# Differential attention: a unit's transposes move to right behind the next unit's scores

## The chip, the core and the metric

The kernel is one program on one core of a Trainium2 chip. The metric is the device time of one launch, in microseconds (us). The core has a matmul engine (TensorE, PE in the profile; its weight loads are listed apart as PEld), a vector engine (VectorE, DVE), an activation engine (ScalarE, ACT), GpSimd (POOL) and a queue engine (SyncE, SP). They run side by side, each works through its own instructions in order, and they wait for one another by semaphores: counters that one engine raises and another waits for.

## The reference

Two transformer blocks of two layers each run one after the other on 256 tokens of width 1024. The change lies in the second layer of the first block, in its differential attention: 8 heads, each with two sets of queries and keys of width 64 and one set of values of width 128. 256 own tokens ask, and 256 own plus 256 context tokens (512 keys) answer.

```python
def diff_attention(h_lat, h_ctx, w_qkv, lam, subln_g, w_o, lam_init, want_ctx):
    ...
    def attend(q, k, v):
        s = jnp.einsum('bqhjd,bkhjd->bhjqk', q, k).astype(jnp.float32) * scale
        p = jax.nn.softmax(s, axis=-1)
        a = p[:, :, 0] - lam_full * p[:, :, 1]
        return jnp.einsum('bhqk,bkhe->bqhe', a.astype(v.dtype), v)
```

Ahead of it come three projections (`q, k, v = jnp.split(h @ w_qkv, 3, axis=-1)`) and a rotation of queries and keys by position; behind it a norm per head and the output projection.

## The kernel before

Every large projection is done as three matmuls of split operands (`mm3`, lines 2449 to 2453: rest of the weights, rest of the activations, and the high parts of both). The weights come in chunks of 128 x 2048 through a ring of three slots. ScalarE cuts the high part out of each chunk (`split_hi`, line 787) and VectorE makes the rest (`split_lo`, line 1345).

**Tiles.** The projection of the attention is a list of tiles, `QKV`: for each of four chunks of columns two q tiles (256 tokens wide), two k tiles (512 wide) and four v tiles (256 wide), 24 matmuls each. Between them stand two "rope" tiles, one matmul with a permutation (line 2863), whose product VectorE needs to rotate q or k. From the second chunk on the order is q0, q1, k0, rope q, k1, v0, rope k, v1, v2, v3. Tile i goes into one of two banks in turn, so TensorE waits ahead of it (`o_free`) until VectorE has copied tile i - 2 out.

**Units.** The attention itself is 16 units, one per head and half of the tokens. It runs between the tiles of the next chunk. A unit u passes through:

- `scores(u)`, TensorE, line 2703: 2 matmuls of 512 columns into ps_g or ps_u (four records in the profile)
- `maximum(u)`, VectorE, line 1719, then `exp(u)`, ScalarE, line 994 (signals at_e)
- `normalise(u)`, VectorE, lines 1736 to 1743: reciprocal, factor of the second set, scaling, and the difference of both sets, which writes the probabilities (signals at_p)
- `flip(u)`, TensorE, line 2712: 4 transposes of the probabilities; waits for at_p of this unit and at_c of the unit before
- `copy(u)`, ScalarE, line 982, out of the bank (signals at_c), `values(u)`, TensorE, line 2726: 4 matmuls (eight records), and `result(u)`, VectorE, line 1748

**Order.** It is written out by hand in `diff_attention` of each engine. Behind the tiles that are no rope tiles and not q0, q1, k0, k1, v0 of the first chunk stands a slot; two slots make a unit's step. In the even slot 2u TensorE does `values(u - 2)` and `scores(u)`, VectorE copies the slot's tile and then does `normalise(u - 1)` and `maximum(u)`, ScalarE does `exp(u)`. In the odd slot 2u + 1 TensorE does `flip(u - 1)`, ScalarE `copy(u - 1)`, and VectorE copies the tile and does `result(u - 2)`. So the even slots 2 to 24 (u = 1 to 12) stand behind v3 of the first chunk; then behind q1, k1, v1 and v3 in turn; the last, slot 24, behind v1 of the last chunk. The odd slots 3 to 25 stand behind q0, k0, v0 and v2. In slot 25 TensorE also does `scores(13)`; slot 26 has an order of its own (`values(11)`, `flip(12)`, `scores(14)`), and the rest follows behind the last tile.

VectorE's order in a step, with q0 to v3 in the place of the tile that it copies, is for example: copy k1, `normalise(2)`, `maximum(3)`; copy v0, `result(1)`, `split_lo`, the rotation of k (lines 1757 to 1759); copy v1, `normalise(3)`, `maximum(4)`; copy v2, `result(2)`; copy v3, and so on.

Of the kernel before, what the change touches and what calls it, by code (L numbers as in the profile page):

```python
# [199 lines left out]
def freed(tiles):  # L200

    return BANKS + tiles
# [73 lines left out]
def build(nc, W, ADA, AW, CB, XT, MEMT, VEC, CST, PM, BT, REL, LAM, W0B, LORA, GUP, OUT, stop=None):  # L276
# [13 lines left out]
    with ExitStack() as ctx:  # L290
# [319 lines left out]
        def qkv_slot(i):  # L610

            kind, c, j = QKV[i]
            if (kind, j) not in QKV_SLOT:
                return None
            s = QKV_SLOT[kind, j]
            return 8 * c + s if s < 3 else 8 * (c - 1) + s if c else None

        def qkv_last(i):

            return i + 1 == len(QKV) or QKV[i + 1][0] in "qkv" and QKV[i][0][-1:] != QKV[i + 1][0] and (QKV[i][0], QKV[i + 1][0]) not in (("rope q", "k"), ("rope k", "v"))  # L620
# [1815 lines left out]
        def _(pe):  # L2436
# [4 lines left out]
            def chunk(n, i=None, per=SLOTS):  # L2441

                pe.wait_ge(w_lo, n + 1 if i is None else i * per + (n + 1))
                return n % SLOTS

            def weights(s, cols_):
                return (whi[:, s, :].rearrange("p (k n) -> p k n", n=cols_), wlo[:, s, :].rearrange("p (k n) -> p k n", n=cols_))
# [7 lines left out]
            def keep_clock(n, bank):  # L2455

                for _ in range(n):
                    mm(bank, ones, cst[:, 0:bank.shape[-1]], start=True, stop=True)
# [233 lines left out]
            def attention(a):  # L2692
                U = ATT[a]

                def scores(u):
                    g, unit = AT0[a] + u, U[u]
                    if g >= 2:
                        pe.wait_ge(at_e, g - 1)
                    if g >= AT0[1] + 3 and is_mem(g):
                        pe.wait_ge(at_y, g - 2)  # L2700
                    bank = att_scores(g)
                    for (rows, b, c), q, k in unit["scores"]:
                        ins = mm(bank[rows, b, c], q, k, start=True, stop=True)  # L2703
                    ins.then_inc(at_s, 1)

                def flip(u):
                    g, unit = AT0[a] + u, U[u]
                    pe.wait_ge(at_p, g + 1)
                    if g:
                        pe.wait_ge(at_c, g)  # L2710
                    for b in range(unit["nb"]):
                        ins = nc.tensor.transpose(att_flip(g, b), probs[g % 2][:, b * 128:(b + 1) * 128], ident)  # L2712
                    ins.then_inc(at_t, 1)

                def values(u):
                    g, unit = AT0[a] + u, U[u]
                    pe.wait_ge(at_c, g + 1)
                    if g < DIFF_UNITS:
                        pe.wait_ge(o_free, freed(QKV_T0 + QKV_V[u // 4] + 1))
                    if g >= 2:  # L2720
                        pe.wait_ge(at_y, g - (g >= DIFF_UNITS))
                    elif g:
                        pe.wait_ge(at_y, g)
                    nb = unit["nb"]
                    for b in range(nb):
                        ins = mm(att_out(g)[unit["rows"]], unit["v"][b], probs_t[a][g % 2][:, b, :], start=b == 0, stop=b == nb - 1)  # L2726
                    ins.then_inc(at_o, 1)

                return scores, flip, values
# [109 lines left out]
            def diff_first():  # L2839

                n = FIRST["qkv", 0]
                ready = split_input(NTOK)
                w = [weights(chunk(n + b), 256) for b in range(2)]
                for i in range(4):
                    pe.wait_ge(o_free, QKV_T0 + i + 1)
                for part, half in enumerate(HALVES):
                    for k in range(KT):
                        ready(k + KT * part)
                        for i in range(2 * part, 4) if part else range(4):
                            b, c = i // 2, slice(i % 2 * 128, i % 2 * 128 + 128)  # L2850
                            ins = mm3(qkv_bank(i)[:, half], (w[b][0][:, k, c], w[b][1][:, k, c]), (hh[:, k, half], hl[:, k, half]), k == 0, k == KT - 1)
                            if k == KT - 1 and part == b:
                                ins.then_inc(mm_done, 1)

            def diff_tile(i, w):

                kind, c, j = QKV[i]
                out, s = qkv_bank(i), slice(j * 128, (j + 1) * 128)
                pe.wait_ge(o_free, QKV_T0 + i + 3)
                if kind[:4] == "rope":  # L2860
                    made = QKV.index(("q", c, 1) if kind == "rope q" else ("k", c, 1))
                    pe.wait_ge(o_free, freed(QKV_T0 + made + 1))
                    mm(out.rearrange("p (a n) -> p a n", a=2), C("perm"), rope_input(kind, c), start=True, stop=True).then_inc(mm_done, 1)
                    return
                for k in range(KT):
                    if kind == "v":
                        ins = mm3(out[:, 0:256], (hh[:, k, s], hl[:, k, s]), (w[0][:, k, :], w[1][:, k, :]), k == 0, k == KT - 1)
                    else:
                        N = NX if kind == "q" else NTOK
                        ins = mm3(out[:, 0:N], (w[0][:, k, s], w[1][:, k, s]), (hh[:, k, 0:N], hl[:, k, 0:N]), k == 0, k == KT - 1)  # L2870
                ins.then_inc(mm_done, 1)

            def diff_attention():

                scores, flip, values = attention(0)
                diff_first()
                n = FIRST["qkv", 0] + 2
                w = weights(chunk(n), 256)
                for i in range(4, len(QKV)):
                    diff_tile(i, w)  # L2880
                    slot = qkv_slot(i)
                    if slot is not None:
                        u, odd = slot // 2, slot % 2
                        if slot == 26:
                            values(11)
                            flip(12)
                            scores(14)
                        elif odd and u:
                            flip(u - 1)
                        elif not odd:  # L2890
                            if u >= 2:
                                values(u - 2)
                            if u % 4 == 0:
                                pe.wait_ge(ro_done, 2 * (u // 4) + 2)
                            scores(u)
                        if slot == 25:
                            scores(13)
                    if qkv_last(i) and i + 1 < len(QKV):
                        n += 1
                        w = weights(chunk(n), 256)  # L2900
                pe.wait_ge(o_free, freed(QKV_T0 + len(QKV)))
                values(12)
                flip(13)
                scores(15)
                subln_sum(0, 0, 6)
                values(13)
                keep_clock(1, ps_o[:, 3, :])
                flip(14)
                values(14)
                keep_clock(1, ps_o[:, 3, :])  # L2910
                flip(15)
                subln_back(0, 0, 6)
                values(15)
                subln_sum(1, 6, 8)

            def subln_sum(part, h0, h1):

                pe.wait_ge(c_late, 16)
                pe.wait_ge(sl_sq, part + 2)
                if part:  # L2920
                    pe.wait_ge(at_e, DIFF_UNITS)
                for h in range(h0, h1):
                    ins = mm(subln_sums[part][0:40, 0:NX], C("sel8", 47)[:, 7 - h:47 - h], squares_at(h, h + 1), start=h == h0, stop=h == h1 - 1)
                ins.then_inc(sl_sum, 1)

            def subln_back(part, h0, h1):

                pe.wait_ge(sl_inv, part + 1)
                if part == 0:
                    pe.wait_ge(at_e, DIFF_UNITS)  # L2930
                for h in range(h0, h1):
                    ins = mm(SUBLN_BACK[h // 2][:, NX * (h % 2):NX * (h % 2 + 1)], C("spread", 1024)[32:40, 128 * h:128 * (h + 1)], subln_rows[part], start=True, stop=True)
                    if h % 2:
                        ins.then_inc(sl_back, 1)
# [203 lines left out]
            scores, flip, values = attention(1)  # L3138
# [350 lines left out]
```

## Time and profile before

| what | us |
|---|---|
| time before, median of 3 runs | 2749.72 |
| the three runs | 2748.23, 2751.78, 2749.72 |
| the profiled execution's own time | 2743.61 |
| span from its first to its last instruction | 2742.0 |
| TensorE busy in the span | 2684.7 (98%) |
| VectorE, ScalarE, GpSimd busy | 2044.7, 1013.3, 145.7 |
| diff attention between the first and the last tile that the change touches | about 1207 to 1325 from the span's start |

A row of the timeline gives start and duration in us, engine, line, operation, what it writes and reads, its shape, how many records are taken together, and in brackets how long the engine was idle before it and what it waited for. TensorE's records overlap: a wide matmul of 256 columns has a duration of 0.28 us, but the next starts 0.12 us behind it. Durations of TensorE are modelled; starts are what to count with.

### The profile page before, as it was taken

Reading aid. Unit: us, or ns where it says so; the run is one execution under the profiler, and the core shown is the slowest. Engines: PE = TensorE matmul, PEld = TensorE weight load, DVE = VectorE, ACT = ScalarE, POOL = GpSimd, SP = SyncE. Lnnn points to the kernel's source line nnn. Section 1 sums busy time; section 2 is a strip of 40 time slices with the busy share of each in tenths; the row PEclk is TensorE's granted clock in tenths of the full one; section 3 lists DMA queues with packets and bytes.
Section 4 is the critical chain, followed back from the end, with each engine's and each line's share of the span. In section 5 each row is a group of like instructions: output and inputs, shape, how many; then the busy total and the mean of one; then the engine's idle time right before and its main releaser. Section 6 shows DMA issues by size and latency. Waiting matters only on the chain.

```text
span 2742.0 us, 49156 instructions
## 1 busy us (share of the span) xinstructions
PE 2684.7 (98%) x19338; PEld 2382.2 (87%) x19338; DVE 2044.7 (75%) x3105; ACT 1013.3 (37%) x1173; POOL 145.7 (5%) x206
## 2 busy tenths in 40 slices
PE   7999999999999999999999999998999999999999
PEld 5888878888888888888799999987799989997999
DVE  6799987777787677776766786767877776676777
ACT  4222234222242222243353453553144444344543
POOL 1011111000010000000010000000000010000000
PEclk9999999999999999999999999999999999999999
DMA  9355532444434333422144444531044555443354
GB/s 363 139 194 195 195 148 85 167 162 153 153 115 153 138 138 139 164 95 78 62 180 184 183 154 184 190 123 48 34 175 184 187 158 184 184 175 79 135 193 178
DMA packets 68707, 421.44 MB, mean 154 GB/s; under 512 B 7672, under 2 KB 8824, under 8 KB 26592
## 3 DMA queue, kind: packets, MB, share of 16 engines
q1 hardware_dynamic: 48176, 343.36, 33.8%
q0 software_dynamic: 20432, 76.69, 8.9%
q8 instruction: 71, 1.16, 0.2%
q14 instruction: 28, 0.23, 0.0%
HBM read 418.95 MB, written 1.07 MB: 153 GB/s over the span
## 4 chain that ended last, share of the span: by engine, by line
PE 91%; DVE 6%; ACT 1%; issue 1%; DMA 0%; SPq 0%; ACTq 0%; DVEq 0%
PE ps_o L2451 11%; PE ps_o L2453 11%; PE ps_o L2452 11%; PE ps_g L2451 8%; PE ps_u L2451 8%; PE ps_u L2453 8%; PE ps_u L2452 8%; PE ps_g L2453 8%; PE ps_g L2452 8%; DVE wlo L1345 1%; PE ps_o L2726 1%; PE ps_o L2712 0%; PE ps_o L3229 0%; ACT whi L787 0%; PE ps_u L2703 0%
## 5 line engine op out<-in xcount | busy, mean ns | idle before, releaser
L787 ACT ACTIVATE whi<-wraw 128x2048 fp32r<-128x2048 f32 x314 | 599.0, 1911 | 759.2 <-PE ps_u L2453 340.7
L1345 DVE TENSOR_TENSOR wlo<-wraw,whi 128x2048 fp32r<-128x2048 f32 x310 | 702.5, 2287 | 113.4 <-ACT whi L787 113.0
L2451 PE MATMUL ps_g<-hh,wlo 128*128 128x256 f32 (+1 forms) x1448 | 461.4, 319 | 2.9 <-DVE hl L1416 2.1
L2451 PE MATMUL ps_u<-hh,wlo 128*128 128x256 f32 (+1 forms) x1448 | 459.8, 318 | 0.0
L2453 PE MATMUL ps_g<-hh,whi 128*128 128x256 f32 (+1 forms) x1448 | 459.5, 317 | 0.0
L2453 PE MATMUL ps_u<-hh,whi 128*128 128x256 f32 (+1 forms) x1448 | 459.4, 317 | 0.0
L2452 PE MATMUL ps_g<-hl,whi 128*128 128x256 f32 (+1 forms) x1448 | 459.0, 317 | 0.0
L2452 PE MATMUL ps_u<-hl,whi 128*128 128x256 f32 (+1 forms) x1448 | 459.0, 317 | 0.0
L2451 PE MATMUL ps_o<-ah,wlo 128*128 128x256 f32 (+1 forms) x1360 | 433.7, 319 | 4.3 <-DVE x L1456 4.3
L2453 PE MATMUL ps_o<-ah,whi 128*128 128x256 f32 (+1 forms) x1360 | 432.8, 318 | 0.0
L2452 PE MATMUL ps_o<-al,whi 128*128 128x256 f32 (+1 forms) x1360 | 432.3, 318 | 0.0
L1456 DVE SCALAR_TENSOR_TENSOR x<-ps_o,gcol,x 128x256 f32<-128x256 f32 x640 | 280.5, 479 | 113.4 <-PE ps_o L2453 108.7
L2451 PEld LDWEIGHTS ps_g<-hh,wlo 128*128 128x128 f32 x1448 | 272.5, 188 | 27.6 <-issue 6.7
L2451 PEld LDWEIGHTS ps_u<-hh,wlo 128*128 128x128 f32 x1448 | 272.5, 188 | 20.7 <-issue 1.4
L2453 PEld LDWEIGHTS ps_g<-hh,whi 128*128 128x128 f32 x1448 | 272.5, 188 | 19.4
L2453 PEld LDWEIGHTS ps_u<-hh,whi 128*128 128x128 f32 x1448 | 272.5, 188 | 19.3
L2452 PEld LDWEIGHTS ps_u<-hl,whi 128*128 128x128 f32 x1448 | 272.5, 188 | 19.2
L2452 PEld LDWEIGHTS ps_g<-hl,whi 128*128 128x128 f32 x1448 | 272.6, 188 | 19.0
L2451 PEld LDWEIGHTS ps_o<-ah,wlo 128*128 128x128 f32 x1360 | 255.7, 188 | 25.1 <-DVE x L1456 3.3
L2452 PEld LDWEIGHTS ps_o<-al,whi 128*128 128x128 f32 x1360 | 255.7, 188 | 18.6
L2453 PEld LDWEIGHTS ps_o<-ah,whi 128*128 128x128 f32 x1360 | 255.7, 188 | 18.7
L907 ACT ACTIVATE ah<-tsq 128x512 fp32r<-128x512 f32 (+1 forms) x85 | 66.6, 784 | 425.4 <-PE ps_o L2453 413.9
(531 smaller groups left out, 3724.8 us busy)
## 6 DMA issues: line engine op xcount, KB each, us to landing
wraw<-in_W SPq DMA_DIRECT2D x315, 1024.0 KB, 4.8
scr<-in_ADA POOLq DMA_DIRECT2D x126, 512.0 KB, 4.3
scr<-in_AW SPq DMA_DIRECT2D x5, 1024.0 KB, 25.9
big<-in_AW SPq DMA_DIRECT2D x4, 1024.0 KB, 15.9
scr<-bias_rows POOLq DMA_DIRECT2D x8, 384.0 KB, 8.8
x<-in_XT SPq DMA_DIRECT2D x1, 2048.0 KB, 8.0
x<-in_MEMT POOLq DMA_DIRECT2D x2, 1024.0 KB, 7.2
cst<-in_CST POOLq DMA_DIRECT2D x1, 1511.5 KB, 7.4
```

Source lines behind the costliest of these rows:

```text
L787: nc.scalar.activation(whi[:, n % SLOTS, :], wraw[:, n % SLOTS, :], ACT.Copy).then_inc(w_hi, 1)
L907: nc.scalar.activation(dst[:, :, 0:N], tmp[:, :, 0:N], ACT.Copy).then_inc(a_hi, 1)
L1345: tt_(wlo[:, n % SLOTS, :], wraw[:, n % SLOTS, :], whi[:, n % SLOTS, :].bitcast(f32), sub).then_inc(w_lo, 1)
L1456: ins = stt(x[:, d, HALVES[j]], src[:, HALVES[j]], gate(d, j), x[:, d, HALVES[j]], mult, add)
L2451: mm(out, a[1], b[0], start=first, stop=False)
L2452: mm(out, a[0], b[1], start=False, stop=False)
L2453: return mm(out, a[0], b[0], start=False, stop=last)
L2726: ins = mm(att_out(g)[unit["rows"]], unit["v"][b], probs_t[a][g % 2][:, b, :], start=b == 0, stop=b == nb - 1)
```

## The change

The turn of a unit's probabilities, `flip(u - 1)`, leaves the odd slots 3 to 25 (12 of them, u = 1 to 12) and stands in the even slot 2u, one tile sooner, right behind `scores(u)`. Nothing else is edited; VectorE, ScalarE, GpSimd and SyncE have the same instructions in the same order.

```diff
                             scores(14)
-                        elif odd and u:
-                            flip(u - 1)
                         elif not odd:
                             if u >= 2:
                                 values(u - 2)
                             if u % 4 == 0:
                                 pe.wait_ge(ro_done, 2 * (u // 4) + 2)
                             scores(u)
+                            if u:
+                                flip(u - 1)
                         if slot == 25:
                             scores(13)
```

TensorE in slot 4 (unit 2) before: the last matmul of tile q1, values(0), scores(2), and the first of tile k0.

```order
L2453 MATMUL ps_o<-hh,whi 128x256
L2726 MATMUL ps_o<-hid,scr 128x128 [waits o_free,at_c]
L2726 MATMUL ps_o<-hid,scr 128x128 x3
L2703 MATMUL ps_g<-scr 128x512 [waits at_e]
L2703 MATMUL ps_g<-scr 128x512
L2451 MATMUL ps_o<-hh,wlo 128x512 [waits o_free,w_lo]
L2452 MATMUL ps_o<-hl,whi 128x512
```

The same place in the changed kernel:

```order
L2726 MATMUL ps_o<-hid,scr 128x128 [waits o_free,at_c]
L2726 MATMUL ps_o<-hid,scr 128x128 x3
L2703 MATMUL ps_g<-scr 128x512 [waits at_e]
L2703 MATMUL ps_g<-scr 128x512
L2712 MATMUL ps_o<-cst,tsq 128x128 [waits at_c,at_p]
L2712 MATMUL ps_o<-cst,tsq 128x128 x3
L2451 MATMUL ps_o<-hh,wlo 128x512 [waits o_free,w_lo]
```

Four transposes (flip(1)) now stand between the scores and the next wide tile, and they wait for at_p, which normalise(1) of the same slot signals.

TensorE one tile later, between tile k0, the rope tile of q and tile k1, before:

```order
L2453 MATMUL ps_o<-hh,whi 128x512
L2712 MATMUL ps_o<-cst,tsq 128x128 [waits at_c,at_p]
L2712 MATMUL ps_o<-cst,tsq 128x128 x3
L2863 MATMUL ps_o<-scr,cst 128x512 [waits o_free]
L2451 MATMUL ps_o<-hh,wlo 128x512 [waits o_free]
```

And in the changed kernel:

```order
L2452 MATMUL ps_o<-hl,whi 128x512
L2453 MATMUL ps_o<-hh,whi 128x512
L2863 MATMUL ps_o<-scr,cst 128x512 [waits o_free]
L2451 MATMUL ps_o<-hh,wlo 128x512 [waits o_free]
L2452 MATMUL ps_o<-hl,whi 128x512
```

The transposes are gone from there; the rope matmul follows the wide tile directly, and tile k1 behind it waits, as before, for the copy of tile k0.

## Rows read from the trace of the kernel before

**Rows 1.** The page's busy times and shares.

```profile
PE 2684.7 (98%) x19338; PEld 2382.2 (87%) x19338; DVE 2044.7 (75%) x3105; ACT 1013.3 (37%) x1173; POOL 145.7 (5%) x206
```

**Rows 2.** Chain that ended last: start, us, what; one step of each kind.

```profile
1206.86 1.06 PE ps_u L2703 x4
...
1210.99 0.44 PE ps_o L2712 x4
...
1222.37 0.86 PE ps_o L2863 x2
```

**Rows 3.** Timeline, PE: start, us, engine, line; scores(1) and the wide tile behind it.

```profile
1206.79 1.13 PE L2703 MATMUL ps_u<-scr 64*128 64x512 f32 x4
1207.85 0.39 PE L2451 MATMUL ps_o<-hh,wlo 128*128 128x256 f32 x1
1208.07 0.28 PE L2452 MATMUL ps_o<-hl,whi 128*128 128x256 f32 x1
```

**Rows 4.** Timeline, DVE: the last operation of normalise(0), (1) and (2).

```profile
1208.14 0.75 DVE L1743 SCALAR_TENSOR_TENSOR tsq<-tsq,cols 128x512 f32<-128x512 f32 x1
...
1215.58 0.75 DVE L1743 SCALAR_TENSOR_TENSOR tsq<-tsq,cols 128x512 f32<-128x512 f32 x1
...
1230.25 0.75 DVE L1743 SCALAR_TENSOR_TENSOR tsq<-tsq,cols 128x512 f32<-128x512 f32 x1
```

**Rows 5.** Timeline, PE: scores(2), scores(3) and scores(4).

```profile
1215.12 1.13 PE L2703 MATMUL ps_g<-scr 64*128 64x512 f32 x4
...
1229.52 1.13 PE L2703 MATMUL ps_u<-scr 64*128 64x512 f32 x4
...
1238.70 1.13 PE L2703 MATMUL ps_g<-scr 64*128 64x512 f32 x4
```

**Rows 6.** Timeline, DVE: from the copy of tile v0 to normalise(3).

```profile
1233.75 0.42 DVE L1773 COPY scr<-ps_o 128x256 f32<-128x256 f32 x1 [1.61 <-PE ps_o L2453]
...
1238.41 0.41 DVE L1773 COPY scr<-ps_o 128x256 f32<-128x256 f32 x1
...
1239.65 0.75 DVE L1743 SCALAR_TENSOR_TENSOR tsq<-tsq,cols 128x512 f32<-128x512 f32 x1
```

**Rows 7.** Timeline, DVE: the copy of tile q1 in unit 6.

```profile
1254.55 0.42 DVE L1769 TENSOR_SCALAR scr<-ps_o 128x256 f32<-128x256 f32 x1 [0.49 <-PE ps_o L2453]
```

**Rows 8.** Timeline, all engines: tile k0's copy, rope q, and tile k1's first weights.

```profile
1221.97 0.69 DVE L1771 COPY scr<-ps_o 128x512 f32<-128x512 f32 x1 [4.46 <-PE ps_o L2453]
...
1222.21 1.02 PE L2863 MATMUL ps_o<-scr,cst 128*128 128x512 f32 x2
...
1222.72 0.19 PEld L2451 LDWEIGHTS ps_o<-hh,wlo 128*128 128x128 f32 x1 [0.31 <-DVE scr L1771]
```

**Rows 9.** Timeline: a flip of the memory attention that waited, and what it waited for.

```profile
1878.05 0.35 DVE L1739 TENSOR_SCALAR tsq<-tsq,cols 128x256 f32<-128x256 f32 x1
...
1878.46 0.33 PE L2712 MATMUL ps_u<-cst,tsq 128*128 128x128 f32 x1 [0.37 <-DVE tsq L1739]
```

**Rows 10.** Timeline, PE: a wide tile that started behind a wait.

```profile
1191.79 0.36 PE L2451 MATMUL ps_o<-whi,hl 128*128 128x256 f32 x1 [0.52 <-DVE scr L1771]
1191.98 0.28 PE L2452 MATMUL ps_o<-wlo,hh 128*128 128x256 f32 x1
```

**Rows 11.** Timeline, ACT and PE: from exp(13) to values(12).

```profile
1326.73 0.69 ACT L994 ACTIVATE tsq<-ps_u,cols 128x512 f32<-128x512 f32 x1 [2.33 <-DVE cols L1719]
...
1328.07 1.91 ACT L787 ACTIVATE whi<-wraw 128x2048 fp32r<-128x2048 f32 x1
1329.87 0.59 ACT L982 ACTIVATE hid<-ps_o 128x512 f32<-128x512 f32 x1
...
1330.56 1.13 PE L2726 MATMUL ps_o<-hid,scr 128*128 128x128 f32 x8 [0.28 <-issue]
```

**Rows 12.** Windows: stretch, us, busy by engine, granted clock, DMA share, GB/s.

```profile
1343.10:1346.50 3.40, 2.25 (x15) 1.66 (x14) 2.79 (x6) 1.89 (x3) 0.00 (x0) 1.00 0.00 0
1346.50:1349.90 3.40, 3.21 (x11) 1.90 (x12) 2.74 (x4) 0.47 (x1) 0.00 (x0) 0.51 0.02 5
```

## The prediction

> **What bounds the kernel now.** I read the busy times first: TensorE is busy for 98% of the span [rows 1], so a microsecond that it loses is a microsecond of the kernel unless something late gives it back. Then the chain of waits: through the stretch that the change touches it runs on TensorE from tile to tile, with the narrow work between tiles as its own steps, 1.06 us for a unit's scores, 0.44 us for a flip, 0.86 us for a rope matmul [rows 2]. Then the timeline of each engine, for one question: when is a unit's probability tile ready, and when will TensorE now ask for it? Before the change a whole tile (24 wide matmuls, 2.9 us or more) lay between the two, and no flip of these waited.
>
> **What the change does to TensorE.** No instruction is added or removed. Two blocks of narrow work per two tiles become one, and the flip asks for its input one tile sooner. What the flips cost themselves (12 x 0.44) stays.
>
> *Joining the blocks.* Scores followed by a wide tile cost 1208.07 - 1206.79 = 1.28 us to the second wide matmul, which is 1.16 us beyond the pace of 0.12 us [rows 3]; the chain gives 1.06 for the matmuls alone. If a flip follows the scores at once instead, the flip starts somewhere between 0.96 and 1.06 us behind their start (no row of this stretch has that pair; 1.06 is where the wide matmul starts, 0.10 less is my bound since the flip's weights may load sooner). So a joined pair saves 0.10 to 0.20 us, 1.2 to 2.4 us for 12, if the probabilities are there.
>
> The Trainium skill (TensorE: Matmul & The Clock Gate, LDWEIGHTS) gives a weight load as its columns over 1.2 GHz, 107 ns for 128 columns; by that, as an estimate, one exposed load saved per joined pair would be 1.3 us in all, inside that bound. The trace has 0.19 us for the load of a wide matmul [rows 8], and the sum doesn't rest on either.
>
> *The wait.* They are not there. normalise(u - 1) is done by VectorE in the same slot, behind the copy of that slot's tile, while TensorE does values(u - 2) and scores(u). normalise(0) ends at 1208.14 + 0.75 = 1208.89, 2.10 us behind the start of scores(1) [rows 3, 4]. For unit 2 the distance is 1216.33 - 1215.12 = 1.21 us, for unit 3 it is 1231.00 - 1229.52 = 1.48 us, for unit 4 it is 1240.40 - 1238.70 = 1.70 us [rows 4 to 6]. The pattern repeats: units 5, 6, 9 and 10 are like 2 (v3 and q1 tiles, copied in 0.42 us), 7 and 11 like 3 (k1 tiles, copied in 0.69 us), 8 and 12 like 4. The smallest distance, 1.21, is above 1.06, so every one of the 12 flips waits. A flip that waited for VectorE in the memory attention started at 1878.46, 0.06 us behind the end of the operation (1878.05 + 0.35) [rows 9]; I take that. So the flip starts at distance + 0.06 behind the scores, where the scores cost 1.16 us before, and a unit loses distance + 0.06 - 1.16:
>
> - unit 1: 2.10 - 1.10 = 1.00 us
> - units 2, 5, 6, 9, 10: 1.21 - 1.10 = 0.11 us each, 0.55 us
> - units 3, 7, 11: 1.48 - 1.10 = 0.38 us each, 1.14 us
> - units 4, 8, 12: 1.70 - 1.10 = 0.60 us each, 1.80 us (more below)
>
> Behind the waiting flip stands the next wide tile, whose weights and banks are ready; it is the tile that pays. VectorE and ScalarE lose nothing by it, but nothing on them is late either, so nothing is bought.
>
> *What the flip covered where it stood.* Three places.
>
> (a) Between v0 and v1. Through the v0 slot and the rotation VectorE works without a pause from 1233.75 on: its copy of v1 at 1238.41 has no wait ahead of it, so VectorE was behind there [rows 6]. Its end is fixed from the end of tile v0. TensorE's way from v0 to scores(4) is now 0.44 us shorter, since the flip has left it, so the distance from scores(4) to the end of normalise(3) grows by 0.44. Units 4, 8, 12: 3 x 0.44 = 1.32 us more. In the q0 slot VectorE also does a split, but it had 0.49 us to spare ahead of q1's copy in unit 6 [rows 7], just over 0.44, and more in the others.
>
> (b) Between k0 and k1. Tile k1 waits for the copy of tile k0, 1221.97 + 0.69 = 1222.66, and its first weight load starts 0.06 us behind that, at 1222.72 [rows 8]. Under the flip and the rope matmul this is hidden: the rope started at 1222.21 and needs 0.86. Now the rope starts 0.44 earlier, is done at about 1222.64, and the copy is as late as before. A wide matmul that waited stood 0.19 us ahead of its second one where the pace is 0.12 [rows 10], so such a tile starts in effect about 0.1 us behind its wait, at 1222.82: 0.18 us of the 0.44 is lost. Three such places: 0.54 us. Between v0 and v1 the copied tile is only 256 wide (0.42 us) and the copy is done before the rope is.
>
> (c) The end. values(12) started at 1330.56, behind copy(12) on ScalarE, which ended at 1329.87 + 0.59 = 1330.46; that copy stands directly behind a split of weights (1328.07), which stands behind exp(13), which waited for maximum(13) on VectorE [rows 11]. All of this hangs on the end of the tile in slot 25, v2. The flip that leaves the place behind that tile lets TensorE reach values(12) 0.44 us earlier, and there it waits: 0.44 us not gained.
>
> **Sum.** 1.00 + 0.55 + 1.14 + 1.80 + 1.32 + 0.54 + 0.44 = 6.79, so 6.8 us. The profiled execution took 2743.61 us (span 2742.0 and 1.6 around it), so it would be 2750.4. Its time is 6.1 us below the median of the runs shown, 2749.72; on that median the change makes 2756.5. Nothing behind the attention is short of anything that these 6.8 us would let run ahead and keep: the chain is TensorE again.
>
> **Unknown costs.** The waited flip may cost more than the 0.44 of one that ran on: 0 to 0.1 us each, by the wide matmul that waited [rows 10], up to +1.2 us; I take 0, as the flip's own loads start with it [rows 9]. (a) to (c) may be cheaper than worked out, down to nothing: -2.3 us, which leaves +4.5.
>
> **The rivals.**
>
> 1. *The couplings (a) to (c) don't hold* and only the direct waits count: 1.00 + 0.55 + 1.14 + 1.80 = 4.5 us, 2754.2. For it: (b) and (c) rest on starts in one execution. Against: the orders are fixed and VectorE's rows have no pause. Chance 0.13.
>
> 2. *The clock falls in a wait.* Before, a stretch in which TensorE was busy for 2.25 of 3.40 us, with scores-like and values-like narrow work in it, was followed by one of 3.40 us at a granted clock of 0.51 [rows 12], the lower of the two levels, 1.2 GHz. Around units 4, 8 and 12 the changed kernel has a bit over 1 us of idling among narrow work, at unit 1 as much among wide tiles. Each fall costs up to half of 3.4, 1.7 us: one or two make 6.8 + 1.7 to 6.8 + 3.4, 2758.2 to 2759.9. Against: the rest of each such step is dense wide work. Chance 0.14.
>
> 3. *The probabilities are ready in time*, and joining pays: not slower. It decides at one place, the end of normalise(u - 1): if that lies less than 1.0 us behind the start of scores(u), the flip runs on and the change gives 1.2 to 2.4 us, less the 0.98 of (b) and (c), so 2749.7 - 0.2 to 2749.7 - 1.4: 2748.3 to 2749.5. For it only that the operations before normalise aren't touched; against it, four measured distances of 1.21 to 2.10. Chance 0.03.
>
> **How the numbers follow.** The forecast, 2756.5, has the remaining 0.70. About 0.2%, 5.5 us, is what a measurement of this kernel can tell from no change; the three runs alone lie 3.5 us apart. The forecast of 6.8 lies 1.3 us above that bound, so some 0.12 of its 0.70 would still be measured as no change. With 0.13 of rival 1 and 0.02 of rival 3 that is 0.27 for within 0.2%; 0.58 of the forecast and 0.14 of rival 2 make 0.72 for slower, and 0.01 of rival 3 is kept for faster by that much. The range takes in rival 1 with the spread of the runs at its lower end (2754.2 - 1.5 = 2752.7) and two falls of the clock at its upper (2760).
>
> **What would show it.** TensorE idle ahead of line 2712, released by line 1743, 12 times, by about 1.0 us at unit 1, 0.15 at units 2, 5, 6, 9, 10, 0.4 at 3, 7, 11 and 0.8 to 1.1 at 4, 8, 12. Tile k1's first weights still 0.06 us behind the end of k0's copy. Idle ahead of values(12) 0.7 us in place of 0.28. Starts behind the attention some 6.8 us later, with the granted clock at 1.00 from unit 1 to unit 12. It is wrong if the flips don't wait, if VectorE's normalise starts at another distance from the tile's end than before, or if the median moves by less than 4 or more than 10 us.

## The result

The changed kernel took 2759.45 us (median of 11 runs, 2754.26 to 2762.92), the kernel before 2748.72 us beside it (11 runs, 2746.20 to 2752.24). The ratio is 1.0036, with a 95% interval of 1.0028 to 1.0044: 7.7 to 12.1 us slower. In a second series, on another occasion, the ratio was 1.0025 (1.0015 to 1.0034). The mean of the two ratios is 1.003, 8.4 us. Forecast were 6.8 us, and a median of 2756.5. The first series' median lies inside the range of 2752.7 to 2760, near its upper end; its interval of the difference lies above 6.8 us, that of the second (4.1 to 9.3 us) takes it in.

The profiled execution of the changed kernel took 2759.92 us, span 2757.9. Its busy times tell little: TensorE was busy for 2692.1 us, 98% of the span as in [rows 1]. What tells is the stretch from the start of scores(1) to values(12), which holds all 12 moved flips. Windows of that stretch, before and then after (stretch, us, busy by engine and records, granted clock, DMA share, GB/s):

```profile
1206.79:1330.56 123.77, 123.49 (x794) 102.34 (x793) 82.22 (x135) 45.43 (x75) 0.00 (x0) 1.00 0.25 92
```

```profile
1209.28:1340.65 131.37, 124.70 (x793) 101.80 (x793) 82.67 (x136) 44.15 (x75) 0.00 (x0) 1.00 0.24 87
```

The stretch is 7.60 us longer, with the same work in it: TensorE was idle for 0.28 us in it before and for 6.67 us after. That is 6.39 of the 7.60 us; the other 1.21 us stand as busy time, since the modelled ends of some records reach over a wait. Its clock stood at 1.00 in both.

Who waits, in the changed kernel (waits, about 1206 to 1345: engine, line waited for, us in total, times, longest):

```profile
PEld ps_o L2712 <- DVE tsq L1743: 15.2, 12, 1.9
...
PE ps_o L2712 <- DVE tsq L1743: 4.6, 7, 1.0
```

All 12 flips now wait for the last operation of normalise. In the same query on the kernel before there is no row of line 2712 that waits for line 1743. The matmul row counts 7 waits and not 12, because at units 2, 5, 6, 9 and 10 the gap is hidden in the modelled end of the scores' last record; the row of the weight loads has all 12.

**Unit 1 and unit 2.** Timeline after, the rows that answer to [rows 3, 5]:

```profile
1209.28 1.13 PE L2703 MATMUL ps_u<-scr 64*128 64x512 f32 x4
1211.44 0.66 PE L2712 MATMUL ps_o<-cst,tsq 128*128 128x128 f32 x4 [1.04 <-DVE tsq L1743]
1211.85 0.37 PE L2451 MATMUL ps_o<-hh,wlo 128*128 128x256 f32 x1
1212.06 0.29 PE L2452 MATMUL ps_o<-hl,whi 128*128 128x256 f32 x1
...
1218.67 1.13 PE L2703 MATMUL ps_g<-scr 64*128 64x512 f32 x4
```

And VectorE's end of normalise, to be held against [rows 4]:

```profile
1210.63 0.75 DVE L1743 SCALAR_TENSOR_TENSOR tsq<-tsq,cols 128x512 f32<-128x512 f32 x1
1219.13 0.75 DVE L1743 SCALAR_TENSOR_TENSOR tsq<-tsq,cols 128x512 f32<-128x512 f32 x1
```

The distances are those of before: 1211.38 - 1209.28 = 2.10 us, 1219.88 - 1218.67 = 1.21 us. The flip starts 0.06 us behind the end, as in [rows 9]. From the flip to the second wide matmul it is 1212.06 - 1211.44 = 0.62 us, where a flip behind a wide tile needed 0.56 before (1210.82 to 1211.38): the flip in its new place costs 0.06 us more.

**Unit 4.** VectorE is behind by the rotation there [rows 6]. After:

```profile
1242.58 0.69 DVE L1759 TENSOR_TENSOR scr<-scr,hid 128x512 f32<-128x512 f32 x1
...
1243.32 1.13 PE L2703 MATMUL ps_g<-scr 64*128 64x512 f32 x4 [0.21 <-DVE scr L1759]
...
1244.42 0.75 DVE L1743 SCALAR_TENSOR_TENSOR tsq<-tsq,cols 128x512 f32<-128x512 f32 x1
...
1245.23 0.66 PE L2712 MATMUL ps_o<-cst,tsq 128*128 128x128 f32 x4 [0.78 <-DVE tsq L1743]
```

Scores(4) start 0.21 us late, because they wait for the rotation of k (`ro_done`), and the flip then waits 0.78 us more. From the start of scores(4) to the end of normalise(3) it is 1245.17 - 1243.32 = 1.85 us, against 1.70 before. The wait on the rotation is one that the prediction had not named.

**Between k0 and k1**, the rows that answer to [rows 8] (timeline, all engines):

```profile
1225.89 1.02 PE L2863 MATMUL ps_o<-scr,cst 128*128 128x512 f32 x2
...
1226.10 0.69 DVE L1771 COPY scr<-ps_o 128x512 f32<-128x512 f32 x1 [5.03 <-PE ps_o L2453]
...
1226.84 0.19 PEld L2451 LDWEIGHTS ps_o<-hh,wlo 128*128 128x128 f32 x1 [0.75 <-DVE scr L1771]
```

The copy ends at 1226.79 and the weights of k1 start at 1226.84, as predicted. The second wide matmul stands at 1227.18, 1.29 us behind the rope matmul's start. Before, from the flip's start at 1221.78 to that matmul at 1223.30, it was 1.52 us. So taking the flip away gave 0.23 us and not 0.44.

**The end.** ScalarE and TensorE, to be held against [rows 11]:

```profile
1338.16 1.91 ACT L787 ACTIVATE whi<-wraw 128x2048 fp32r<-128x2048 f32 x1
1339.96 0.59 ACT L982 ACTIVATE hid<-ps_o 128x512 f32<-128x512 f32 x1
```

```profile
1340.65 1.13 PE L2726 MATMUL ps_o<-hid,scr 128*128 128x128 f32 x8 [0.72 <-issue]
```

values(12) is idle for 0.72 us ahead of it in place of 0.28: the 0.44 that the flip left free behind v2 are waited away here.

**Outside the stretch** the two profiled executions differ by 8.3 us more (15.9 in the span against 7.6). The table splits two traces of each kernel; the second pair is from the experiments below. The last column is the part of the span in which TensorE had the lower of its two clock levels; no part of it lies ahead of values(12).

| trace | start to scores(1) | scores(1) to values(12) | values(12) to the end | span | at the lower clock |
|---|---|---|---|---|---|
| before | 1206.79 | 123.77 | 1411.4 | 2742.0 | 17.1 |
| before, second | 1207.52 | 123.77 | 1414.9 | 2746.2 | 27.3 |
| after | 1209.28 | 131.37 | 1417.3 | 2757.9 | 30.7 |
| after, second | 1208.94 | 131.44 | 1413.7 | 2754.1 | 23.9 |

The middle column is the change. The column behind it goes with the lower clock: with half of the last column taken off, as an estimate of what the clock cost, it is 1402.9, 1401.2, 1401.9 and 1401.8 us, the same for both kernels within 1.7 us. The first trace of before, on which the page of the kernel before rests, was one with little time at the lower clock. The column ahead is 1.4 to 2.5 us longer in the changed kernel's traces, and that difference is there from TensorE's very first matmul, which starts at 16.25 and 17.00 us before and at 19.13 and 18.13 us after, more than 1180 us ahead of the first moved flip.

### The profile page after: what moved, and what is told of

Read it like the earlier page. It is cut to its first block, busy times and chain, and to the rows that moved or that the text cites. A ratio compares the mean times of both kernels' runs of the same rounds, so it can differ in the third digit from the quotient of the medians.

```text
span 2757.9 us, 49156 instructions
## 1 busy us (share of the span) xinstructions
PE 2692.1 (98%) x19338; PEld 2387.5 (87%) x19338; DVE 2045.4 (74%) x3105; ACT 1011.9 (37%) x1173; POOL 145.8 (5%) x206
## 4 chain that ended last, share of the span: by engine, by line
PE 89%; DVE 8%; ACT 1%; issue 1%; DMA 0%; SPq 0%; ACTq 0%; DVEq 0%
PE ps_o L2451 11%; PE ps_o L2452 11%; PE ps_o L2453 11%; PE ps_g L2451 8%; PE ps_u L2451 8%; PE ps_u L2452 8%; PE ps_u L2453 8%; PE ps_g L2452 8%; PE ps_g L2453 8%; DVE wlo L1345 2%; PE ps_o L2712 1%; PE ps_o L2726 1%; PE ps_o L3229 1%; PE ps_g L2478 0%; DMA x<-in_XT 0%
```

## The experiments

All times are from the start of scores(1) to values(12) of each kernel's trace unless another is named; the two traces of each main kernel agree in it to 0.07 us, so it tells apart what the kernels' times, with a spread of some 6 to 12 us, can't. The granted clock is 1.00 over this stretch in every trace. The runs for which no ratio is given have one execution each.

**The kernel before, again.** No edit.

> The kernel before, unchanged, for its spread, its granted clock run by run, and a second trace. The two traces so far give 7.6 us more from the start of scores(1) to values(12) in the changed kernel, while its median is 10.7 us higher. Theory A (the 3 us left over is chance: which short stretches fall to the lower clock differs from run to run, and the one profiled run of before had few of them): the mean granted clock of these runs spreads over 0.994 to 0.997 as that of the changed kernel does, and a second trace shows other stretches at the lower clock. Theory B (the change brings more clock falls behind the attention): these runs stay at 0.996 to 0.997, and the ratio to the kernel before is 1.000 all the same.

Measured: ratio 1.0001 (0.9991 to 1.0010), 123.77 us in the stretch. Its mean granted clock over 12 executions was 0.9948, from 0.993 to 0.996; that of the changed kernel's first 11 was 0.9945, from 0.994 to 0.996. Its trace has 27.3 us at the lower clock in place of 17.1. That is theory A: how much of the time the clock is low differs between executions of one kernel, and the means of the two kernels differ by no more than the executions do.

**The changed kernel, again.** No edit.

> The changed kernel, unchanged, to narrow down its cost: its median was 10.7 us above that of before, while its trace has 7.6 us more from the start of scores(1) to values(12). Theory A (the rest is chance in the start and in the granted clock): the same 7.6 us there again, mean granted clock within 0.001 of the kernel before, and together with the earlier runs a cost that comes down towards 7.6 to 9 us (ratio 1.0028 to 1.0033). Theory B (something behind the attention also gets slower): 10 us again, and a piece behind values(12) that is longer than in both traces of before by the same amount.

Measured: ratio 1.0025 (1.0015 to 1.0034), 131.44 us in the stretch, mean granted clock 0.9952 over 11 executions against 0.9949 for the 21 of the kernel before beside it. Values(12) to the end is 1413.7 us, between the two traces of before. Theory A again. What can be said of the whole: the traces' 7.6 us lie just below the first series' interval (7.7 to 12.1) and inside the second's (4.1 to 9.3). As an estimate, the clocks 0.9952 and 0.9949 are worth 0.8 us in favour of the changed kernel in the second series, so its 6.9 us would be 7.7 us at one clock.

One thing doesn't fit chance so well. Directly behind the attention TensorE was at the lower clock for 10.2 us in all three traces that have the whole change (the two of this kernel and the one with copy(12) first, below), and for 6.8 us in both traces of before. Half of 3.4 us is 1.7 us. The other kernels below have 3.4 to 13.7 us there, and the mean clocks above show no such difference, so it is not shown to belong to the change; nor is it ruled out.

**The same order on TensorE, with the probabilities ready.** VectorE does normalise(u) in the odd slot, for u up to 11. The split of weights from the v0 slot moves behind the maximum of the next slot, out of the rotation's way:

```diff
                         elif odd:
                             if u >= 2:
                                 result(u - 2)
+                            if slot < 25:
+                                normalise(u)
                         elif not odd:
-                            if u:
-                                normalise(u - 1)
                             maximum(u)
...
-                    if i in QKV_SPLIT:
+                    if i in [t + 2 * (QKV[t][0] == "v" and QKV[t][2] == 0) for t in QKV_SPLIT]:
```

> The changed order on TensorE, and VectorE does normalise(u) one tile sooner, in the odd slot 2u + 1 behind result(u - 2), for u up to 11 (and the weights' split of the v0 slots stands behind maximum of the next slot, so that the rotation is as early as before). Theory A (the flips cost what they wait for VectorE): normalise(u - 1) now ends over 2 us ahead of the end of scores(u), no flip waits, the flip starts 0.96 to 1.06 us behind the scores, and the kernel is at or below the one before: -0.2 to -1.4 us from scores(1) to values(12), ratio 0.9995 to 1.0005. Theory B (one long block of narrow work costs more by itself than two short ones, by refilling or by the clock): the wait is gone, but 3 us or more of the 10 stay.

Measured: ratio 0.9996 (0.9985 to 1.0008). VectorE's normalise(1) and TensorE's slot 4 in this kernel (timeline; its lines are numbered one higher from line 1745 on):

```profile
1214.72 0.75 DVE L1743 SCALAR_TENSOR_TENSOR tsq<-tsq,cols 128x512 f32<-128x512 f32 x1
```

```profile
1217.14 1.13 PE L2704 MATMUL ps_g<-scr 64*128 64x512 f32 x4
1218.20 0.66 PE L2713 MATMUL ps_o<-cst,tsq 128*128 128x128 f32 x4
```

normalise(1) ends at 1215.47, 1.67 us ahead of scores(2), and the flip starts 1.06 us behind the scores, without a wait. All 12 do so. From scores(1) to scores(12) the kernel takes 112.53 us, where before takes 112.35 and the changed kernel 118.69. So up to scores(12) the waits are nearly the whole of it: take them away, and 6.2 of 6.3 us are back. What is not there either is the gain from joining the blocks. The 112.53 hold three places between k0 and k1 that lose 0.21 each, by the rows of the main kernels; the eleven joined pairs make up for 0.45 of these 0.63 us, which is 0.04 us a pair. The prediction's bound was 0.10 to 0.20. The flip does start at the late end of that bound, 1.06, and it costs 0.06 more than on its own, wait or no wait: from its start to the second wide matmul behind it it is 1218.93 - 1218.20 = 0.73 us at unit 2 here and 1220.67 - 1219.94 = 0.73 in the changed kernel, where it waited. Why it costs 0.06 more behind scores, no run tells.

Over the stretch to values(12) 0.2 to 1.4 us less than before was expected and 1.6 us more is measured (125.38). From scores(12) to values(12) this kernel is 1.4 us slower than before, since the split of weights that was moved out of the rotation's way now stands in VectorE's row ahead of the copy of v2.

**VectorE's edit alone**: both hunks of the diff above, with the flips where the kernel before has them.

> The same edit of VectorE's order on the kernel before, flips where they were. It tells what the edit of VectorE costs or gives by itself. Both theories: no flip waits either way, within 0.1% of before (2.7 us). If it costs more, that amount has to be taken off the run with the joined order.

Measured: ratio 1.0003 (0.9994 to 1.0012); scores(1) to scores(12) 112.35 us, as before to the hundredth, and the same 1.4 us at the end. The moved split starts at 1323.86 there and takes 2.29 us, and the copy of v2 stands at 1326.06, 18.00 us behind scores(1), where it stood 16.57 us behind it before. The edit of VectorE costs nothing up to scores(12), so the run above can be read as it stands.

**Only units 4, 8 and 12.** `flip(u - 1)` stands behind `scores(u)` for these three, in the odd slot for the others.

```diff
+                        elif odd and u % 4:
+                            flip(u - 1)
...
-                            if u:
+                            if u and u % 4 == 0:
                                 flip(u - 1)
```

> Only three of the twelve flips are moved, those of units 4, 8 and 12, which stand behind tile v1, where VectorE is behind with the rotation. Theory A (waits, with the flip's old place covering VectorE): from scores(1) to values(12) 3 x (0.60 + 0.44 + 0.06) + 0.44 = 3.7 us more, half of the whole. Theory C (every moved flip costs the same): 3/12 of 7.6, 1.9 us. By the ratio 1.0014 against 1.0007.

Measured: 126.22 us, 2.45 more; ratio 1.0010 (0.9999 to 1.0020). Neither 3.7 nor 1.9. The expectation had a slip: the flip that stood between v0 and its rope tile and covered VectorE there is flip(2), which unit 3 moves, not flip(3). Without the three times 0.44 the same terms give 3 x 0.66 + 0.44 = 2.4. This was worked out behind the run; the next two test it.

**Only units 3, 7 and 11.** The same kind of edit for these three.

> Only the flips of units 3, 7 and 11 are moved. They are the ones that stood between v0 and its rope tile, while VectorE was busy up to the copy of v1. Measured from scores(1) to values(12), where before has 123.77 us. By the direct waits alone: 3 x (0.38 + 0.06) = 1.3 us. By the cover: the 0.44 us that TensorE saves behind v0 is partly taken back at scores(4), (8), (12), which wait for the rotation of k (1759) to end, by about 0.2 us each: 1.9 us. The flips of units 4, 8 and 12 keep their old place, so no flip is there to wait for VectorE's late normalise, and the full 0.44 is not lost.

Measured: 126.01 us, 2.24 more, above both 1.3 and 1.9; the cover is larger than the 0.2 us a place that was expected. The row of scores(4) in this kernel (timeline):

```profile
1240.94 1.13 PE L2703 MATMUL ps_g<-scr 64*128 64x512 f32 x4 [0.22 <-DVE scr L1759]
```

The wait for the rotation is there with no moved flip behind it. From scores(3) to scores(4) it is 9.91 us here and 9.18 before, 0.73 more, of which 0.38 + 0.06 are the flip's own; the other 0.29 are the cover.

**Both groups together.**

> The flips of units 3, 7, 11 and of 4, 8, 12 together; apart they gave 2.24 and 2.45 us more from scores(1) to values(12). If the cover of point (a) is charged in full at scores(4), (8) and (12), which wait for the rotation, the two add up: 4.7 us. If the flip behind them waits for the same late VectorE too, each of the three places costs some 0.15 us on top, as the whole change shows it: 5.1 us.

Measured: 128.89 us, 5.12 more; apart they make 4.69. The 0.43 between, 0.14 at each of the three places, is what the flip of units 4, 8 and 12 waits for the late VectorE. So the 0.44 of cover is paid in two pieces, 0.29 at the scores, 0.14 at the flip.

**Only units 2, 6 and 10.** `flip(u - 1)` behind `scores(u)` for these three alone, by the same kind of edit.

> Only the flips of units 2, 6 and 10 are moved, the ones that stood between tile k0 and its rope tile. It tests point (b), that tile k1 is held by the copy of k0 once the flip no longer stands there. Measured from scores(1) to values(12), before 123.77 us. With (b): direct wait 0.11, flip behind scores 0.06 and k1 held for 0.21 each: 3 x 0.38 = 1.1 us more. Without (b): 3 x 0.17 = 0.5 us.

Measured: 124.87 us, 1.10 more. The rows between k0 and k1 (timeline, all engines):

```profile
1223.64 0.69 DVE L1771 COPY scr<-ps_o 128x512 f32<-128x512 f32 x1 [5.04 <-PE ps_o L2453]
...
1224.38 0.19 PEld L2451 LDWEIGHTS ps_o<-hh,wlo 128*128 128x128 f32 x1 [0.75 <-DVE scr L1771]
```

Point (b) holds: without it 0.5 was expected.

**The changed kernel with copy(12) ahead of the last split** on ScalarE.

```diff
-                    if qkv_last(i):
+                    if qkv_last(i) and i + 1 < len(QKV):
                         split_hi(n + SLOTS)
                         n += 1
...
                         if slot == 26:
                             copy(12)
+                            split_hi(n + SLOTS)
                             exp(14)
```

> The changed kernel, and ScalarE does copy(12) ahead of the last split of weights. It tests point (c), that values(12) is held by ScalarE's order and not by TensorE. If so, the idle ahead of values(12), 0.72 us, goes, and scores(1) to values(12) is 130.7 us in place of 131.37. If it is held by something else, nothing moves.

Measured: 130.63 us. values(12) starts at once behind scores(14):

```profile
1339.15 1.13 PE L2704 MATMUL ps_g<-scr 64*128 64x512 f32 x4
1340.21 1.16 PE L2727 MATMUL ps_o<-hid,scr 128*128 128x128 f32 x8
```

The stretch is 0.74 us shorter than in the changed kernel, of which 0.28 were idle in the kernel before too. Point (c) holds, with its size.

**Joining where it should pay.** normalise early for u up to 10, the flips of units 1, 3, 4, 5, 7, 8, 9 and 11 joined, copy(12) first. The last of the moved splits stays where it was.

> The best that can be made of joining: VectorE does normalise(u) one tile sooner for u up to 10, the flips of units 1, 3, 4, 5, 7, 8, 9 and 11 stand behind the scores, those of units 2, 6 and 10 stay between k0 and its rope tile, where they cover the copy of k0, that of unit 12 stays behind v2, and ScalarE does copy(12) ahead of the last split. By the run with all flips joined and no waits, a flip behind scores costs 0.49 us against 0.44 on its own, and a joined pair saves 0.05 to 0.1 us net: 8 x 0.05 = 0.4 us, and 0.3 us at values(12). From scores(1) to values(12) 123.0 to 123.3 us against 123.77, in the kernel's time nothing that can be measured (ratio 0.999 to 1.0005). If joining is worth what the bound in the prediction allowed (0.10 to 0.20 each), it is 121.9 to 122.7.

Measured: 123.47 us, 0.30 less than before, where 123.0 to 123.3 was expected. Ratio 0.9999 (0.9990 to 1.0008). It is no faster than the kernel before by anything that can be measured. Up to scores(12) it takes 112.40 us, 0.05 more than before; the gain lies behind that, 0.28 of it in the idle time ahead of values(12) that copy(12) first takes away. Joining gives 0.03 to 0.04 us a pair here too (scores(1) to scores(2) 8.29 against 8.33), but at scores(12) it is lost again (timeline; lines there are numbered 1 to 4 higher than in the kernel before):

```profile
1320.14 1.13 PE L2707 MATMUL ps_g<-scr 64*128 64x512 f32 x4 [0.22 <-DVE scr L1760]
```

From scores(11) to scores(12) it takes 9.44 us against 9.18. The flip of unit 11 has left its place, the split ahead of the rotation has not, and the scores wait for the rotation as at unit 4 in the run on units 3, 7 and 11. So this kernel is not quite the best that joining can give: with the flip of unit 11 left in its old place too it would gain some 0.2 us more, an estimate from these rows (9.44 - 9.18 - 0.04) that no run shows.

## Why the prediction was right, and where it was short

The sum was 6.8 us; the trace shows 7.60. Its mechanism holds, and one of its terms was too small. Regrouped by what the runs can tell apart:

| units | forecast | measured | how measured |
|---|---|---|---|
| 1, 5, 9 | 1.22 | 1.38 | 7.60 - 5.12 - 1.10 |
| 2, 6, 10, with (b) | 0.87 | 1.10 | a run of its own |
| 3, 4, 7, 8, 11, 12, with (a) and (c) | 4.70 | 5.12 | a run of its own |
| all | 6.79 | 7.60 | |

- **The bound.** TensorE alone. Right: its chain of tiles sets the stretch, and VectorE and ScalarE matter only where TensorE waits for them.
- **The waits.** All 12 flips wait for normalise, with the distances read from the kernel before (2.10, 1.21, 1.48) and 0.06 us behind its end. Right to 0.01 us, and for units 4, 8 and 12 right in total.
- **The flip's own cost** was put at 0.44 us and the extra for one that waited at 0, out of a range of 0 to 0.1. It is 0.06, twelve times, 0.7 us. This is the term that was too small, and it is most of the difference of 0.8. The rows given for taking 0, [rows 9], show the start of one transpose and nothing of what followed it. The reason that was weighed for it, a restart behind a wait, was not the one: the flip costs 0.06 more behind scores even if it doesn't wait.
- **(a), the cover of VectorE.** Its total holds (0.29 + 0.14 = 0.43 against 0.44). Its place was told wrong: the distance from scores(4) to the end of normalise(3) was to grow by 0.44 and grew by 0.15; two thirds of the cover are paid by the scores, which wait for the rotation.
- **(b)** was 0.21 and not 0.18, **(c)** 0.44 as worked out; both were tried by themselves.
- **Rival 1**, that the couplings don't hold, falls with the runs on units 3, 7, 11 and on 2, 6, 10 and with the one on copy(12). **Rival 2**, that the clock falls in a wait, falls for the 12 units: the granted clock is 1.00 over the stretch in both traces of the changed kernel. (The window of 3.40 us in [rows 12] holds values and small matmuls of line 2932, but no scores.) Whether the stretch of lower clock behind the attention gets longer by the change stays open. **Rival 3** named the right deciding point; with the probabilities ready the kernel is level with before (0.18 us slower up to scores(12)), not faster by its 0.2 to 1.4 us, because a joined pair saves 0.04 us and not 0.10 to 0.20.
- **The kernel's time.** The first series has 7.7 to 12.1 us more, the second 4.1 to 9.3. That the rest of the first series' 9.9 us is chance is argued from the clock, the starts and the repeats, not shown. The forecast of slower by more than 0.2% came true in the first series (1.0028 at least); the second alone would not have told it (1.0015 at least). The first series' median lies 10.7 us above the one beside it, the second's 8.3. That the first came within 0.6 us of the upper end of the range is no term of the sum: the traces' 7.6 us on 2748.72 would be 2756.3. That this is almost the forecast median is partly luck: the sum was 0.8 us too small, and the median that it was added to 1.0 us above that of the 11 runs.

A sentence of the Trainium skill bore on the joining: TensorE: Matmul & The Clock Gate, LDWEIGHTS, gives 107 ns for loading 128 columns, by which one exposed load saved per pair would have been an estimated 1.3 us in all. The run with the flips joined and not waiting shows 0.04 us a pair net, 0.5 us for 12: the flip starts 0.10 us sooner than the wide tile's first matmul counted in the pace, and gives 0.06 of it back. So the whole 1.3 us are not there to gain; whether the 0.10 us are a weight load, no run here shows.

## What to carry to other kernels

Before a step is moved nearer to what it reads, measure in the trace of before how long after its new neighbour its input is ready, per place: 12 distances, four kinds, told most of the cost here. Then look at what the step covered where it stood. A short block between two long ones may be what gives a late engine or a copy its time, and here a third of the loss came from such places. And try to make the input earlier first: with that done the move cost 0.2 us here in place of 6.3 up to scores(12), but it also showed that the move was worth nothing. If that means moving work of another engine, look at the end of its row too: here the moved split cost 1.4 us there.

## What the runs showed of the hardware that was not expected

- Joining two blocks of narrow matmuls saved 0.04 us a pair, where 0.10 to 0.20 had been read from the starts. Four transposes cost 0.44 us between wide tiles and 0.50 behind scores.
- TensorE had the lower of its two clock levels for 17 to 34 us of the span in each traced execution, in stretches of 3.4 to 10.2 us. They lie near a few places, which recur in most traces whatever the kernel (within 32 us behind values(12), and near 1890, 2475 and 2510 us from the span's start); which of them occur and how long they last differs between executions of one kernel (17.1 and 27.3 us in all in the kernel before). That moves a span by some 5 us with nothing changed.
- The start of scores(1) varied from 1206.8 to 1209.6 us between traces, without any difference in the code ahead of it in the two that lie furthest apart. TensorE's first matmul varies with it, from 16.25 to 19.22 us in these two.
